# Two-layer hybrid encoder on eight cores: the tokens taken in two halves, attention of one half issued beside the dense work of the other

## The chip, the cores and the metric

One Trainium2 chip, eight cores, one program on all of them. Each core computes one of the eight batch elements on its own; the weights are the same for all. The time is the device time of the slowest core in microseconds. Kernel before: median 2806.88 us of three runs (2804.39 to 2817.87).

## The reference, cut to what matters

2064 tokens (16 learned meta tokens and 2048 of the sequence), 1024 channels, two layers, then a final RMSNorm. One layer:

```python
h = rms_norm(x, norm1_g)
q, k, v, u, gate_pre = split(h @ w_in, [512, 1024, 1536, 2048])     # u: pool input, 2048 gate channels
g_pool, g_sb = split(sigmoid(gate_pre + b_gate), 2)
a = pool_mixer(u)                       # trailing means over 2/4/8/16 tokens, minus the token, 4 small maps
s = stick_breaking_attention(q, k, v)   # 8 heads of 64; A[t,s] = beta_ts * prod_{s<j<t} (1 - beta_tj), s < t
x = x + (g_pool * (a @ w_branch_pool) + g_sb * (s @ w_branch_sb)) @ w_out
gt, up = split(rms_norm(x, norm2_g) @ w_ffn_in, 2)                  # 2 x 2816
x = x + (silu(gt) * up) @ w_ffn_out
```

Token t looks at earlier tokens only, in attention and in the pool.

## The kernel before, in words

Tokens are stored in reverse order, so the keys of a query lie at higher columns. Channels are on the partitions, tokens on the free axis. The residual `X` (float32) and the normed `H` (bf16) of all 2064 tokens stay in SBUF. `Prog` (L37) records every operation with what it reads and writes; `op` and `dma` (L94, L103) turn overlaps into semaphore waits. Each engine executes its operations in the order in which the Python code recorded them; that order is written out by hand. Weights come from HBM as float32 through POOL's DMA queue (`wdma`, L299), cast to bf16 on the way. Helpers record nearly everything: `mm` (L264) and `mmx` (L271) matmuls, `act` (L280), `tt` (L283), `stt` (L286), `cp` (L291 on ACT, L293 on DVE).

A layer runs in stages, each over all tokens before the next, in tiles of 512 tokens and one of 16 (`TT`): projections q and u with the pool mixer (`proj_fm`, `proj_u`, `pool_band`), then k and v, then `attention` (L525), then `merge_slab` (gates and branch projections, four weight slabs, L647), `out_proj` (L687) and six `ffn_slab` (L716), each slab over all token tiles, its weights loaded while the slab before it computes. The norms are taken inside `out_proj` and the last `ffn_slab`. The FFN's output is added to `X` once per slab.

`attention` cuts the work into units: one block of 128 queries, one head, one chunk of up to 7 key blocks; 224 units per layer and, in layer 0, eight more of 16 queries. A unit goes through five engines: `prep` (L558) issues the q.k matmuls on PE into one of three PSUM pairs; `core` (L576) lets ACT take the sigmoid in place, DVE scan the running product over the keys (L591), POOL subtract neighbours to get the weights (tt, L283), and SP's queue transpose them by DMA (L608, four buffers); `av` (L610) multiplies with v on PE (L624). Where a query's keys need more than one chunk, DVE copies the last product into `CAR` (L293). The loop at L636 issues `prep` two units ahead and `av` three units behind; nothing but attention is issued in this stage.

Of the kernel before, what the change touches and what calls it, by code (L numbers as in the profile page):

```python
# [11 lines left out]
D = 1024  # L12
# [7 lines left out]
TT = [(512 * i, 512 * (i + 1)) for i in range(4)] + [(2048, 2064)]  # L20
KB = [(128 * j, 128 * j + 128) for j in range(16)] + [(2048, 2064)]
CELL = 16
SUBE = 'pool'
NEG = -30000.0

# [10 lines left out]

class Prog:  # L37
    def __init__(self, nc):
        self.nc = nc
        self.ops = []  # L40
        self.cnt = {}
        self.arenas = {}
        self.alias = {}
# [4 lines left out]
    def _res(self, rs):  # L48
        out = []
        for (an, lo, hi) in rs:  # L50
            if an in self.alias:
                an, off, mul = self.alias[an]
                lo, hi = off + lo * mul, off + hi * mul
            out.append((an, lo, hi))
        return out

    def _record(self, eng, fn, reads, writes, stream, val, skip):
        need = {}
        reads, writes = self._res(reads), self._res(writes)
# [7 lines left out]
        for (an, lo, hi) in writes:  # L67
            A = self.arenas[an]
            c0, c1 = lo // CELL, (hi + CELL - 1) // CELL
            for tab in (A['W'], A['R']):  # L70
                for s, arr in tab.items():
                    v = int(arr[c0:c1].max())
                    if v > need.get(s, 0):
                        need[s] = v
        for s in skip:
            need.pop(s, None)
        for s, v in need.items():
            if s.startswith('E:'):
                assert v <= self.cnt.get(s, 0), ("dependency on a not-yet-issued inc", s, v)
# [14 lines left out]
    def op(self, eng, fn, reads=(), writes=(), inc=True):  # L94
# [3 lines left out]
        need = self._record(eng, fn, reads, writes, stream, val, skip)  # L98
        if inc:
            self.cnt[stream] = val  # L100
        self.ops.append(dict(eng=eng, fn=fn, need=need, inc=inc, dma=None))

    def dma(self, queue, fn, sem, reads=(), writes=()):  # L103
        stream = 'D:' + sem
        val = self.cnt.get(stream, 0) + 16
        need = self._record(queue, fn, reads, writes, stream, val, (stream,))
# [52 lines left out]
class Sub:  # L159
    def __init__(self, tens, off, mul=1):  # L160
        self.tens, self.off, self.mul = tens, off, mul

    def __getitem__(self, idx):
        ps_, cs_ = idx
        ap = self.tens[ps_, self.off + cs_.start * self.mul:self.off + cs_.stop * self.mul]
        return ap.bitcast(F32) if self.mul == 2 else ap

class View:
    def __init__(self, tens, name, off, A, T):
        self.tens, self.name, self.off, self.A, self.T = tens, name, off, A, T  # L170

    def ap(self, a, t0, t1, p0=0, p1=128):
        b = self.off + a * self.T
        return self.tens[p0:p1, b + t0:b + t1]

    def r(self, a, t0, t1):
        b = self.off + a * self.T
        return (self.name, b + t0, b + t1)

def build(depth=DEPTH):  # L180
    nc = bass.Bass("TRN2", target_bir_lowering=False)
    dt = nc.dram_tensor
    xT_d = dt("xT", [D, SEQ], F32, kind="ExternalInput").ap()
    meta_d = dt("metaT", [D, NMETA], F32, kind="ExternalInput").ap()
    prm_d = dt("params", [128, NPC], F32, kind="ExternalInput").ap()
    cst_d = dt("consts", [128, CO], F32, kind="ExternalInput").ap()
    w_in_d = dt("w_in", [DEPTH, D, 4096], F32, kind="ExternalInput").ap()
    pmix_d = dt("pool_mix", [DEPTH, 4, 128, 128], F32, kind="ExternalInput").ap()
    wbp_d = dt("w_branch_pool", [DEPTH, 512, D], F32, kind="ExternalInput").ap()
    wbs_d = dt("w_branch_sb", [DEPTH, 512, D], F32, kind="ExternalInput").ap()  # L190
    wout_d = dt("w_out", [DEPTH, D, D], F32, kind="ExternalInput").ap()
    wfi_d = dt("w_ffn_in", [DEPTH, D, 2 * DFF], F32, kind="ExternalInput").ap()
    wfo_d = dt("w_ffn_out", [DEPTH, DFF, D], F32, kind="ExternalInput").ap()
    y_d = dt("yT", [D, SEQ], F32, kind="ExternalOutput").ap()

    P = Prog(nc)
    with contextlib.ExitStack() as st:
# [4 lines left out]
        Xt = sb("X", 8 * NT, F32)  # L202
        PRM = sb("PRM", NPC, F32)
        ATT = sb("ATT", 20480, BF16)
        Ht = sb("H", 8 * NT, BF16)
        MIX = sb("MIX", 33488, BF16)
# [5 lines left out]
        WB, BW, FW = Sub(ATT, 0), Sub(ATT, 8192), Sub(ATT, 16384, 2)  # L212
        P.alias = dict(WB=('ATT', 0, 1), BW=('ATT', 8192, 1), FW=('ATT', 16384, 2))
        PSB = [st.enter_context(nc.psum_tensor("psb%d" % b, [128, 1024], F32)) for b in range(4)]

        class _Bank:
            def __init__(self, b):
                self.t, self.o = PSB[b // 2], (b % 2) * 512

            def __getitem__(self, idx):  # L220
                ps_, cs_ = idx
                c0 = cs_.start or 0
                c1 = 512 if cs_.stop is None else cs_.stop
                return self.t[ps_, self.o + c0:self.o + c1]

        PS = [_Bank(b) for b in range(8)]
        P.arena('ps', 8 * CELL)
        P.arena('out', CELL)

        X = View(Xt, "X", 0, 8, NT)  # L230
        H = View(Ht, "H", 0, 8, NT)
        Q = View(MIX, "MIX", 0, 4, NT)
        K = View(MIX, "MIX", 8272, 4, NT)
        V = View(MIX, "MIX", 16528, 17, 512)
        A = View(MIX, "MIX", 25232, 4, NT)
        MG = View(MIX, "MIX", 8272, 8, NT)

# [3 lines left out]
        def fw(lo, hi):  # L241
            return FW[:, lo:hi], ('FW', lo, hi)

        def bw(lo, hi):
            return BW[:, lo:hi], ('BW', lo, hi)

        IDENT = CST[:, 0:128]
        NEGM = CST[:, 128:CB]
        NEGONES = CST[:, CO:CO + 128]
        r_cst = ('CST', 0, CB)  # L250
        r_one = ('CST', CO, CO + 128)
# [667 lines left out]
```

How the kernel before makes its waits and increments, by code:

```python
            def run(ename, eng):  # L120
                waited = {}
                for o in ops:
                    if o['eng'] != ename:
                        continue
                    for s, v in o['need'].items():
                        if waited.get(s, 0) < v:
                            eng.wait_ge(sems[s], v)
                            waited[s] = v
                    if o['fn'] is None:
                        continue
                    ins = o['fn'](eng)
                    if o['dma'] is not None:
                        ins.then_inc(sems['D:' + o['dma']], 16)
                    elif o['inc']:
                        ins.then_inc(sems['E:' + ename], 1)
```

## Time and profile before

| | us |
|---|---|
| median of three runs | 2806.88 |
| profiled execution, its own time | 2806.74 |
| span of its slowest core (0) | 2804.7 |
| spans of the eight cores | 2787.2 to 2804.7 |
| PE, DVE, ACT, POOL busy | 2248.5, 1418.0, 730.2, 630.7 |
| mean granted TensorE clock of the cores | 0.816 to 0.819 |

The profile is of one execution. Busy time of an engine counts its instructions; PE and PEld (weight loads) overlap. The granted clock is a share of 2.4 GHz. A matmul's mean ns is longer than its distance from the next one, since matmuls are pipelined. Releasers (what a waiting instruction waited for) are inferred from semaphores. DMA share is the mean busy share of 16 DMA engines, GB/s what they moved (for weights, the bf16 bytes).

### The profile page before, as it was taken

How to read it: one execution, taken by the hardware profiler on the slowest of the kernel's cores; microseconds unless marked ns; L12 is line 12 of the kernel's file. 1: busy time of each engine (PE TensorE's matmuls, PEld its weight loads, DVE VectorE, ACT ScalarE, POOL GpSimd, SP SyncE). 2: the span in 40 equal slices, each digit the busy share in tenths (PEclk: the TensorE clock that was granted, in tenths of full speed). 3: DMA queues.
4: the chain of work that ended last, by engine and by line, in shares of the span. 5: the costliest groups of instructions: out<-in, count | busy, mean ns of one | idle time of the engine just before them, and what ended most of it. 6: DMA issues, size and time to landing. Idle time of an engine off the chain costs nothing.

```text
span 2804.7 us, 37292 instructions; the slowest of 8 cores (2787.2 to 2804.7 us)
## 1 busy us (share of the span) xinstructions
PE 2248.5 (80%) x10905; PEld 973.2 (35%) x11064; DVE 1418.0 (51%) x1840; ACT 730.2 (26%) x1245; POOL 630.7 (22%) x545
## 2 busy tenths in 40 slices
PE   3985665654998899999998866666589999999994
PEld 1442222221444344444444322222134444444441
DVE  3113778885343643333462267888833464433344
ACT  3312333332222211111243233333322321111132
POOL 0003666665000000000000156666610000000000
PEclk9995555555999999999999955555589999999997
DMA  6022545556222222115002044555461322221102
GB/s 160 1 30 44 88 89 97 97 96 101 32 38 38 46 46 46 16 31 77 1 1 31 10 85 85 95 102 98 90 76 23 53 45 46 46 46 19 27 27 94
DMA packets 405714, 159.56 MB, mean 57 GB/s; under 512 B 330128, under 2 KB 391568, under 8 KB 405520
## 3 DMA queue, kind: packets, MB, share of 16 engines
q1 hardware_dynamic: 335968, 96.67, 17.8%
q0 software_dynamic: 69552, 60.51, 15.0%
q8 instruction: 97, 1.59, 0.2%
q14 instruction: 97, 0.79, 0.1%
HBM read 129.51 MB, written 8.39 MB: 49 GB/s over the span
## 4 chain that ended last, share of the span: by engine, by line
PE 66%; DVE 14%; DMA 8%; issue 5%; ACT 4%; POOL 2%; SPq 1%; DVEq 0%; ACTq 0%; POOLq 0%
PE psb L264 57%; DVE ATT L591 11%; PE psb L271 5%; PE psb L624 4%; ACT psb L280 3%; DMA ATT<-ATT 3%; POOL ATT L283 2%; DMA yT<-ATT 2%; DMA X<-xT 2%; DMA ATT<-w_in 1%; DVE MIX L283 1%; SPq L608 1%; DVE H L286 1%; DMA ATT<-w_branch_sb 1%; DVEq L127 0%
## 5 line engine op out<-in xcount | busy, mean ns | idle before, releaser
L283 POOL TENSOR_TENSOR ATT<-ATT 128x768 bf16<-128x768 f32 (+6 forms) x456 | 554.5, 1219 | 339.7 <-DVE CAR L293 197.0
L264 PE MATMUL psb<-H,MIX 128*128 128x512 bf16 (+1 forms) x3098 | 626.5, 357 | 4.9 <-DVE X L283 1.1
L271 PE MATMUL psb<-MIX 64*128 64x512 bf16 (+9 forms) x824 | 330.7, 460 | 328.3 <-DVE ATT L591 325.5
L591 DVE TENSOR_TENSOR_SCAN ATT<-psb,ZF 128x770 f32<-128x770 f32 (+10 forms) x264 | 371.3, 1426 | 188.6 <-ACT psb L280 156.4
L264 PEld LDWEIGHTS psb<-H,MIX 128*128 128x128 bf16 x3168 | 286.5, 98 | 337.3 <-issue 8.9
L283 DVE TENSOR_TENSOR X<-X,psb 128x512 f32<-128x512 f32 (+1 forms) x504 | 308.8, 629 | 156.7 <-PE psb L264 156.5
L280 ACT ACTIVATE psb<-psb 128x770 f32<-128x770 f32 (+6 forms) x456 | 293.0, 671 | 314.1 <-PE psb L271 282.0
L264 PE MATMUL psb<-H,ATT 128*128 128x512 bf16 (+1 forms) x1718 | 355.5, 357 | 11.0 <-DMA ATT<-w_in 7.7
L264 PE MATMUL psb<-MIX 128*128 128x512 bf16 (+1 forms) x1569 | 329.9, 359 | 35.1 <-DVE MIX L283 34.0
L283 DVE TENSOR_TENSOR MIX<-ATT,psb 128x512 bf16<-128x512 f32 (+1 forms) x198 | 124.1, 630 | 453.1 <-PE psb L264 449.3
L280 ACT ACTIVATE ATT<-psb 128x512 f32<-128x512 f32 (+1 forms) x221 | 121.4, 550 | 821.1 <-PE psb L264 799.5
L591 DVE TENSOR_TENSOR_SCAN ATT<-psb,CAR,ZF 128x530 f32<-128x530 f32 (+4 forms) x192 | 282.4, 1522 | 6.9 <-issue 0.4
L264 PE MATMUL psb<-MIX,ATT 128*128 128x512 bf16 (+1 forms) x1138 | 238.9, 358 | 10.9 <-DMA ATT<-w_out 7.6
L271 PEld LDWEIGHTS psb<-MIX 64*128 64x128 bf16 (+1 forms) x824 | 67.1, 101 | 492.3 <-issue 467.2
L264 PEld LDWEIGHTS psb<-H,ATT 128*128 128x128 bf16 x1760 | 158.7, 99 | 195.6 <-issue 20.6
L624 PE MATMUL psb<-ATT,MIX 128*64 128x256 bf16 (+3 forms) x1288 | 180.9, 407 | 52.9 <-DMA ATT<-ATT 52.6
L264 PEld LDWEIGHTS psb<-MIX 128*128 128x128 bf16 x1584 | 142.1, 98 | 215.0 <-issue 61.5
L283 DVE TENSOR_TENSOR ATT<-ATT,psb 128x512 f32<-128x512 f32 (+1 forms) x144 | 90.3, 630 | 235.2 <-PE psb L264 234.7
L299 POOL DMA_DIRECT2D MIX<-w_ffn_in x24 | 21.2, 889 | 747.3 <-PE psb L264 747.3
L280 ACT ACTIVATE ATT<-psb,PRM 128x512 f32<-128x512 f32 (+1 forms) x144 | 91.7, 641 | 258.1 <-PE psb L264 255.5
L264 PEld LDWEIGHTS psb<-MIX,ATT 128*128 128x128 bf16 x1152 | 104.7, 99 | 133.3 <-issue 14.8
L299 POOL DMA_DIRECT2D ATT<-w_in x24 | 21.3, 893 | 567.6 <-PE psb L264 557.7
(38 smaller groups left out, 1012.8 us busy)
## 6 DMA issues: line engine op xcount, KB each, us to landing
MIX<-w_ffn_in POOLq DMA_DIRECT2D x20, 1024.0 KB, 13.0
MIX<-w_ffn_out POOLq DMA_DIRECT2D x10, 1024.0 KB, 19.6
X<-xT SPq DMA_DIRECT2D x4, 2048.0 KB, 35.3
ATT<-w_in POOLq DMA_DIRECT2D x8, 1024.0 KB, 19.7
ATT<-w_in POOLq DMA_DIRECT2D x16, 512.0 KB, 10.2
yT<-ATT SPq DMA_DIRECT2D x32, 256.0 KB, 2.5
ATT<-ATT SPq DMA_TRANSPOSE x456, 2.7
ATT<-w_out POOLq DMA_DIRECT2D x4, 1024.0 KB, 9.3
```

What stands on the lines that cost most here:

```text
L264: P.op('pe', lambda e: e.matmul(out, lhsT=lhsT, rhs=rhs, start=start, stop=stop), reads, writes, inc)
L271: P.op('pe', lambda e: e.matmul(out, lhsT=lhsT, rhs=rhs, start=start, stop=stop, skip_group_check=True), reads, writes, inc)
L280: P.op('act', lambda e: e.activation(out=out, in_=in_, func=func, **kw), reads, writes)
L283: P.op(eng, lambda e: e.tensor_tensor(out=out, in0=in0, in1=in1, op=op), reads, writes)
L286: P.op('dve', lambda e: e.scalar_tensor_tensor(out=out, in0=in0, scalar=scalar, in1=in1, op0=op0, op1=op1), reads, writes)
L299: P.dma('pool', lambda e: e.dma_start(out=out, in_=in_), sem, (), writes)
L591: P.op('dve', lambda e: e.tensor_tensor_scan(out=E, data0=za, data1=zero, initial=init, op0=ALU.mult, op1=ALU.add), r_z + [('ZF', 0, 16)] ...
L608: P.dma('sp', lambda e: e.dma_start_transpose(out=dst, in_=src), 'tw%d' % (u['n'] % 4), [r_w], wr)
L624: P.op('pe', lambda e, out=out, lh=lh, rh=rh, st_=st_, sp_=sp_, hh=hh: e.matmul(out, lhsT=lh, rhs=rh, start=st_, stop=sp_, tile_position=( ...
```

## The change

The sequence is cut into half A (columns 1024 to 2063, the earlier 1040 tokens, meta tokens included) and half B (columns 0 to 1023). Two generators yield work: `attn` gives the attention units of layer 0 A, 0 B, 1 A, 1 B, and `dense` gives everything else in the order shown. Each yields what its next piece reads and writes; the loop at the end asks a model of the engines' times, kept in `Prog` (`t`, `fin`, durations `d`), which piece would be ready, and records attention first, dense work otherwise. Tokens hold pieces back: attention of a half waits for its q projection (`Q`), gates of a half for its attention (`S`). All dense work gets three PSUM banks (eight in the last part), attention two PSUM pairs instead of three and three transpose buffers instead of four. Half A is tiled in three tiles of 346 or 347 columns where the meta tokens are needed, else two of 512.

The weights are packed on the host so that each transfer is contiguous, 2048, 1408 or 1024 elements per partition, in order of use, and pass through a ring of 8192 elements per partition; each half of each layer loads all of them again. `X` holds one half: the other is stored to HBM and loaded back on SP's queue. `H` is kept for all tokens. The FFN runs in two slabs of 11 x 128 channels, not six. Copies out of PSUM go to ACT, the sum of the two gated branches to POOL; silu is taken as sigmoid times value (ACT, ACT, POOL) except in the last part.

```diff
-TT = [(512 * i, 512 * (i + 1)) for i in range(4)] + [(2048, 2064)]
+T3 = [(1718, 2064), (1371, 1718), (1024, 1371)]
+T2 = {'A': [(1536, 2048), (1024, 1536)], 'B': [(512, 1024), (0, 512)]}
+QKV = [('k', 0, 2048), ('k', 1, 2048), ('v', 0, 2048), ('v', 1, 2048), ('q', 0, 2048), ('q', 1, 2048)]
+REST = [('u', 0, 2048), ('u', 1, 2048)]
+for _n in range(8):
+    REST += [('g', _n, 2048), ('b', _n, 1024)]
+REST += [('o', _n, 1024) for _n in range(8)]
+for _s in range(NFC // SLAB):
+    REST += [('i', _s * SLAB + _f, 2048) for _f in range(SLAB)]
+    REST += [('f', _s * 8 + _n, SLAB * 128) for _n in range(8)]
+RING = 8192
...
+    def dma(self, queue, fn, sem, reads=(), writes=(), d=1000.0):
...
+        self.tdma = max(self.tdma, t) + d
+        self.fin.setdefault(stream, []).append(max(self.tdma + 1800.0, t + 2500.0))
...
+        def w_try(force):
...
+            if not force and P.ready([], wr) > max(P.t['pe'], P.t['pool']):
+                return False
+            dst = WR[:, pos:pos + n]
+            src = w_d[l, off:off + 128 * n].rearrange("(p n) -> p n", p=128)
+            P.dma('pool', lambda e: e.dma_start(out=dst, in_=src), 'w%d' % (i % 10), [], wr, d=128 * n * 4 / 330.0)
...
             for u in units:
+                yield ('tok', ('Q', l, h, x))
+                yield u_probe(u)
+                while avq and avq[0]['n'] <= u['ch']['n'] - 2:
+                    av(avq.pop(0))
+                prep(u)
                 core(u)
...
+                def ffn_in(f, tile, s=s):
...
+                    a, ra = stg(k, N)
+                    c, rc = stg(k + 1, N)
+                    b = yield from group([(wsl(pi, kc), H.ap(kc, t0, t1)) for kc in range(8)], [ri] + h_r(t0, t1), N)
...
+                        act(a, ps(b, 0, N), AF.Sigmoid, [psr(b)], [ra], N)
+                        act(c, ps(b, 0, N), AF.Identity, [psr(b)], [rc], N)
+                        tt('pool', a, a, c, ALU.mult, [ra, rc], [ra], N)
+                    b = yield from group([(wsl(pi + 1024, kc), H.ap(kc, t0, t1)) for kc in range(8)],
+                                         [ri] + h_r(t0, t1), N)
+                    tt('dve', M_.ap(f, t0, t1), a, ps(b, 0, N), ALU.mult, [ra, psr(b)], [M_.r(f, t0, t1)], N)
...
+            yield from project(0, 'B')
+            yield from rest(0, 'A', 'sig')
+            yield from project(1, 'A')
+            yield from rest(0, 'B', 'sig')
+            yield from project(1, 'B')
+            load_pmx(1)
+            yield from rest(1, 'A', 'sig')
+            yield ('tok', ('S', 1, 'B'))
+            ps_pool[0] = list(range(8))
+            yield from rest(1, 'B', 'silu')
...
+            now = P.t['pe'] + 60.0
+            cand = []
+            if avq:
+                cand.append((P.ready(*av_probe(avq[0]), skip=('E:pe',)), 'av'))
+            for i in range(2):
+                if heads[i] is not None and heads[i][0] != 'tok':
+                    cand.append((P.ready(*heads[i], skip=('E:pe',)), i))
...
+            pick = [c for c in cand if c[0] <= now]
+            c = pick[0] if pick else min(cand, key=lambda c: c[0])
```

`project` is k, v, q of a half; `rest` is its pool mixer, the wait for `S`, gates and branches (`gate`), output (`outp`), norm, and FFN (`ffn_in`, `ffn_out`). `project(1, 'A')` first waits for attention 0 B, since K, V and Q are used again. `group` is 8 matmuls (4 for a branch, 11 for `ffn_out`) into one PSUM bank; `stg` gives two pairs of staging buffers in turn. A planned order is fixed when the program is built; on the chip each engine still executes its own list in order.

## Rows read from the trace of the kernel before

**Rows 1.** The page: busy time by engine, and PE and its clock in 40 slices of 70 us.
```profile
PE 2248.5 (80%) x10905; PEld 973.2 (35%) x11064; DVE 1418.0 (51%) x1840; ACT 730.2 (26%) x1245; POOL 630.7 (22%) x545
...
PE   3985665654998899999998866666589999999994
...
PEclk9995555555999999999999955555589999999997
```

**Rows 2.** Busy time by stretch, attention stages: stretch, length, engines, PEclk, DMA share, GB/s.
```profile
213.00:680.00 467.00, 272.30 (x1198) 97.71 (x1197) 343.02 (x331) 157.15 (x268) 283.45 (x236) 0.51 0.48 86
1597.00:2035.00 438.00, 266.41 (x1166) 94.22 (x1165) 340.92 (x322) 155.71 (x256) 279.42 (x225) 0.50 0.52 91
```

**Rows 3.** The same view, outside attention (engines: PE, PEld, DVE, ACT, POOL).
```profile
0.00:70.00 70.00, 24.28 (x85) 6.99 (x85) 23.16 (x44) 27.13 (x56) 3.41 (x8) 1.00 0.68 160
...
680.00:1526.00 846.00, 792.62 (x4309) 369.96 (x4384) 349.14 (x610) 188.19 (x336) 31.34 (x38) 0.97 0.24 35
...
2035.00:2704.00 669.00, 643.48 (x2902) 289.02 (x2963) 276.60 (x408) 122.91 (x195) 30.32 (x37) 0.99 0.27 40
2704.00:2804.70 100.70, 57.33 (x245) 24.86 (x247) 44.44 (x64) 30.45 (x45) 0.00 (x0) 0.78 0.23 84
sum 1899.70, PE 1709.80 PEld 781.26 DVE 734.07 ACT 417.39 POOL 67.79; mean PE 284.97 PEld 130.21 DVE 122.35 ACT 69.56 POOL 11.30
```

**Rows 4.** The chain that ended last, by engine, and one dense piece: start, length, what.
```profile
PE 66%; DVE 14%; DMA 8%; issue 5%; ACT 4%; POOL 2%; SPq 1%; DVEq 0%; ACTq 0%; POOLq 0%
...
2061.13 10.74 PE psb L264 x49
```

**Rows 5.** Timeline around two attention units of 770 columns: start, length, engine, line, operation.
```profile
664.54 0.80 PE L271 MATMUL psb<-MIX 64*128 64x512 bf16 x2 [1.37 <-DVE ATT L591]
...
664.74 1.82 DVE L591 TENSOR_TENSOR_SCAN ATT<-psb,CAR,ZF 128x770 f32<-128x770 f32 x1
665.55 0.80 ACT L280 ACTIVATE psb<-psb 128x770 f32<-128x770 f32 x1 [1.38 <-PE psb L271]
666.66 0.15 DVE L293 COPY CAR<-ATT 128x1 f32<-128x1 f32 x1
...
666.83 1.47 POOL L283 TENSOR_TENSOR ATT<-ATT 128x768 bf16<-128x768 f32 x1 [0.70 <-DVE CAR L293]
666.91 1.82 DVE L591 TENSOR_TENSOR_SCAN ATT<-psb,CAR,ZF 128x770 f32<-128x770 f32 x1
```

**Rows 6.** Busy time by stretch: the output projection with its norms; then ten microseconds after a weight wait.
```profile
900.00:1000.00 100.00, 86.54 (x427) 39.22 (x433) 57.88 (x98) 24.68 (x43) 2.53 (x3) 0.95 0.21 32
...
880.00:885.00 5.00, 5.00 (x17) 1.93 (x16) 0.88 (x2) 0.00 (x0) 0.00 (x0) 0.66 1.31 197
885.00:890.00 5.00, 5.00 (x32) 2.40 (x31) 1.87 (x3) 1.47 (x2) 0.00 (x0) 1.00 0.20 37
```

**Rows 7.** Groups by shape (busy, mean ns): a POOL operation of 512 columns, a weight DMA's issue.
```profile
L283 POOL TENSOR_TENSOR ATT<-ATT 128x512 bf16<-128x512 f32 x16 | 16.6, 1039 | 18.6 <-DVE CAR L293 18.6
...
L299 POOL DMA_DIRECT2D MIX<-w_ffn_in x24 | 21.2, 889 | 747.3 <-PE psb L264 747.3
```

**Rows 8.** DMA queues (packets, MB, share of 16 engines), and transposes: us from issue to landing.
```profile
q1 hardware_dynamic: 335968, 96.67, 17.8%
q0 software_dynamic: 69552, 60.51, 15.0%
...
ATT<-ATT SPq DMA_TRANSPOSE x456, 2.7
```

**Rows 9.** Timeline where the first weight loads after attention meet its last transposes; transposes' landing from 660 to 690 us.
```profile
678.07 1.80 POOL L299 DMA_DIRECT2D ATT<-w_in  x2 [0.54 <-POOL ATT L283]
...
681.32 0.94 POOL L299 DMA_DIRECT2D ATT<-w_in  x1
...
686.84 1.38 PE L624 MATMUL psb<-ATT,MIX 128*64 128x256 bf16 x9 [7.05 <-DMA ATT<-ATT]
...
DMA to landing us min/median/max: 2.6/2.7/8.7
```

More of the change, by code:

```diff
@@ new lines, in wget, with wfree, x_pump @@
+        def wget(l, h, k, j):
+            i = widx[(l, h, k, j)]
+            while wstate['next'] <= i:
+                w_try(True)
+            pos, n = wpos[i]
+            return pos, ('WR', pos, pos + n)
+        def wfree(l, h, k, j):
+            i = widx[(l, h, k, j)]
+            wlive[:] = [a for a in wlive if a[0] != i]
+        xq = []
+        def x_pump(force=False):
+            while xq:
+                reads, writes, fn, sem, nb = xq[0]
+                if not force and P.ready(reads, writes) > P.t['pe']:
+                    return
+                xq.pop(0)
+                P.dma('sp', fn, sem, reads, writes, d=nb / 300.0)
@@ L523, in chunks, with geo @@
             return cuts
[L525 to L530 removed]
+        def geo(u):
+            k0, k1 = KB[u['lo']][0], KB[u['ch']['kz'] - 1][1]
+            return k0, k1, k1 - k0 + 2, KB[u['b']][1] - KB[u['b']][0]
@@ L531, in attention @@
+        def attention(l, h):
+            units = []
+            gs = (([8] if l < depth - 1 else []) + [7, 6, 5, 4]) if h == 'A' else [3, 2, 1, 0]
+            for g in gs:
                 bs = [16] if g == 8 else [2 * g, 2 * g + 1]
@@ new lines, in attn @@
+        def attn():
+            for l in range(depth):
+                for h in 'AB':
+                    yield from attention(l, h)
+        P.dma('sp', lambda e: e.dma_start(out=PRM[:, :], in_=prm_d), 'prm', (), [r_prm])
+        P.op('dve', lambda e: e.memset(CST[:, CO:CO + 128], -1.0), (), [r_one])
+        P.op('dve', lambda e: e.memset(ZF[:, :], 0.0), (), [('ZF', 0, 16)])
+        P.op('dve', lambda e: e.memset(Kt[:, 0:16], 0.0), (), [('K', 0, 16)])
+        P.op('dve', lambda e: e.memset(Wt[:, :], 0.0), (), [('W', 0, 3072)])
@@ new lines, in build, with settle, advance @@
+        for k, (t0, t1) in enumerate(T3):
+            x_load_tile('A', 2 + k, t0, t1)
+        x_pump(True)
+        wget(0, 'A', 'k', 1)
+        P.dma('pool', lambda e: e.dma_start(out=CST[:, 0:CO], in_=cst_d[:, 0:CO]), 'cst', [], [('CST', 0, CO)])
+        load_pmx(0)
+        streams = [attn(), dense()]
+        heads = [next(s) for s in streams]
+        def settle(i):
+            while heads[i] is not None and heads[i][0] == 'tok' and heads[i][1] in tokens:
+                advance(i)
+        def advance(i):
+            try:
+                heads[i] = next(streams[i])
+            except StopIteration:
+                heads[i] = None
```

1131 lines of the change are left out of this document (545 added, 586 removed).

## The prediction, made before the changed kernel was run

> **What bounds the kernel now.** I read the page first. PE is busy 80% of the span, but its clock row stands at half in two runs of seven slices [rows 1]: these are the attention stages. So the next view is busy time by stretch. In the two attention stages (467 and 438 us, 905 together) the granted clock is 0.50, that is 1.2 GHz, and PE is busy for 272 and 266 us, 60% of the time; DVE is the busiest with 343 and 341 [rows 2]. Outside them PE is 94 to 96% busy in the long stretches at 0.97 and 0.99, that is 2.4 GHz, and DVE under half [rows 3]. The chain agrees: 66% PE, 14% DVE, 8% DMA; a dense piece of it is 49 matmuls in 10.74 us, 219 ns each [rows 4]. The timeline of an attention unit shows its pace: scan 1.82, carry copy 0.15, the next scan 2.17 us after the last one, while q.k (0.80), sigmoid (0.80) and subtraction (1.47) lie beside it [rows 5]. So the kernel is two programs in turn: PE alone at full clock for 1900 us, and DVE's scan for 905 us with PE waiting at half clock.
>
> **The change, term by term.** *PE work.* Dense work keeps its matmuls: 1710 us [rows 3]. Three tiles of 347 columns instead of two of 512 and one of 16: 219 ns less 213 (512 columns at 2.4 GHz) leaves 6 fixed, so 3 x 150 = 452 against 438 and the small tile; I count nothing, with 15 us either way. Attention's 539 us were taken at half clock [rows 2]; at 2.4 GHz they are about 269. Sum 1979. Whether the clock stays up is a bound: 269 or 539, and half speed for what lies beside it (third rival); I take 269, since a stretch 87% busy ran at 0.95 and after a weight wait the clock was back at 1.00 within ten microseconds [rows 6].
>
> *What lies beside what.* A quarter (half the tokens, one layer) is 427 us of dense PE work. By matmuls per 512 tokens (96 for q, k, v; about 40 for u and pool; 784 for gates, branches, output, FFN) that is 45, 19 and 364 us. Attention of A has 27% of the key columns (36 us of PE, 0.27 x 438 = 118 us of time today), B 73% (98 and 320). In order: k, v and the first q of A with its norms, 39 us, alone. Attention 0 A beside the rest of q, B's projections and A's pool: 114 us of PE against 118 of scans; this stretch is DVE's, and I add 25 us of PE idle. Attention 0 B beside rest 0 A: 462. Project 1 A 45 alone, then attention 1 A beside rest 0 B and project 1 B: 464. Attention 1 B beside rest 1 A: 481. Rest 1 B alone: 383. That is PE's 1979 us again, with 320 us of scans to hide in more than 460, so DVE stops being the bound.
>
> *Ends.* Today PE has 24 us of work in the first 70 [rows 3], 46 idle; three smaller loads and fewer weights before the first matmul, but also three norms before k: between 30 and 65, I take 50. The tail today has 43 us without PE in its last 101 [rows 3]; the last norm now writes into X itself and waits for no staging buffer, but the norm, its stores and their landing remain: 20 to 43, I take 30. So 1979 + 25 + 50 + 30 = 2084.
>
> *Stalls of PE in the planned order.* Alone (467 us) it loses 4% as in 2035 to 2704 [rows 3], 20 us. In the three mixed stretches (1407 us) it waits in order on ACT, DVE, POOL and DMA. No stretch of today is like it; the nearest are that 4% (55 us) and the output projection with its norms, 87% busy, which loses 16% (220 us) [rows 6]. I take 9%, 125 us: closer to the second would be right if the order were written by hand, but a piece is only placed where the model has it ready. Sum 2084 + 20 + 125 = 2229.
>
> *Costed at nothing, and the cover.* DVE in the largest mixed stretch: 0.73 x 342 = 250 of attention, and 234 dense operations of 347 columns at about 0.5 us, 117; 367 in some 500 us. The four FFN slabs saved, 256 adds over the two layers, and the copies moved to ACT lighten DVE where it is not the bound: nothing. POOL: 0.73 x 281 = 205 [rows 2], 90 sums and products at 0.70 (1039 ns for 512 columns) and 68 weight issues at 0.89 [rows 7], in all 328. In order behind a weight issue stand the subtractions; it waits for a ring slot only where PE lags the plan, and then attention waits with it. By the code 280 weight DMAs take the place of 80; if nothing hid them, 200 x 0.89 = 178 us of POOL. Two PSUM pairs: 0.40 + 0.80 + 1.97 and handoffs, some 3.4 us per pair, so 1.7 per unit under the 2.17 of DVE; with a dense group (8 x 0.219 = 1.75) in front of each q.k it is 2.6 per unit, 144 x 2.6 = 374, still inside 500. DMA: weights today 60.5 MB in 15.0% of the span, 0.144 MB/us [rows 8]; the mixed stretch of rest 0 A loads 28.8 MB, 200 us. Transposes of B, 29 MB at 86 / 0.48 = 179 GB/s [rows 2], 163 us; x out and back, 8.5 MB at 160 / 0.68 [rows 3], 36 us. In all 399 of 500: covered, but with little left, and it is second after PE. The x transfers stand on SP's queue ahead of transposes; were one planned 3 us too early, three subtractions would wait for it.
>
> *Transposes meeting weights.* They land after 2.7 us today, almost all without weights beside them [rows 8]. The one collision is after attention: with five weight DMAs issued from 678 to 682 us a transpose took 8.7, and PE stood for 7.05 [rows 9]. A load of 2048 elements (0.52 MB) takes 3.6 us at 0.144 and is wanted every nine, so weights flow 40% of the time; a transpose that meets one load lands by 6.3. Bounds 2.7 and 8.7; mean about 4.1, nearer to the first, since loads come singly. With three buffers a unit takes (landing + 1.47 + 0.3) / 3: 2.0 us at 4.1, 282 for B's 144 units, no cost.
>
> The profiled execution took 2806.74 us, 2 above its span and equal to the median of 2806.88 within 0.2; so the sum gives 2229 + 2, **2230 us**, 577 below.
>
> **Rivals.** *First: the planned order does not fit and PE waits in it.* A product of the FFN passes ACT twice, POOL and DVE: 2 x 0.45 + 0.70 + 0.5 and handoffs, 2.5 us, and up to 0.80 + 1.47 + 1.82 more where an attention operation stands in front on each. PE can run ahead by three banks, 3.6 us with 347 columns. Half of the worst gap of 3 us on 66 products is 99 us, some 30 elsewhere; with 16% for the other stalls the time is 2084 + 20 + 220 + 130 = 2454. For it: every queue is in order, two staging pairs. Against: the model knows these queues, and attention fills gaps. Case: 2310 to 2700.
>
> *Second, ending slower: transposes starve behind the weights.* Place: SP's DMAs in all four attentions, buffers W. If every transpose lands as the one at 678 us did, a unit takes 3.49 us. PE's list was laid out for some 330 us per attention of B, 143 and 150 for A, so the stretch grows by 2 x (144 x 3.49 - 330) + 88 x 3.49 - 143 + 80 x 3.49 - 150 = 638: 2868 us. It decides from a mean landing of 8.3 us, where the extra is 577. For it: rows 9, and weights flow during every attention now. Against: five loads were queued there, and the ring holds four units, one or two of them in use. The Trainium skill, page "DMA: Bandwidth & Descriptors", section "Queues, rings and completion order", has each DMA engine take turns between queues packet by packet. By that rule the packed weights, in pieces of up to 4096 bytes instead of 870, would hold a transpose of 34 packets per engine (157 KB on average, in packets of 288 bytes) for about 15 us while loads are queued, an estimate from that page: 0.4 x 15 + 2.7, a mean landing of about 8.8, and a time near 2890. Rows 9 agree in direction; no run here shows the larger packets.
>
> *Third, also slower: the clock.* Where PE waits so much that it falls to 1.2 GHz, each microsecond of its work costs one more. It decides where 577 of the some 1520 us of work beside attention run at half. For it: 60% busy ran at 0.50 [rows 2]. Against: these stretches need PE over 85% busy.
>
> *Fourth: nothing gained*, because tokens and waits put the halves one after another again: about 2807.
>
> **Chances.** Forecast, 2090 to 2310: 0.60. First rival 0.26. Second 0.09, third 0.03, fourth 0.02. Half a percent, 14 us, is about what a measurement of this kernel can tell from no change. Faster 0.86, same 0.02, slower 0.12. The range reaches from the lower bounds (mixed stalls at 4%, start and tail at their least: 2230 - 70 - 20 - 10 = 2130, less 40 if the small tiles and the attention matmuls, packed between others, cost less than counted) to the middle of the first rival's case: 2090 to 2560; it leaves out 0.14 above for the others and a few hundredths of the first rival.
>
> **What would show it.** Right: PEclk at 0.9 or more in all mixed slices; PE 85 to 95% busy in them; DVE 70 to 75%; the chain over 80% PE; attention 0 B ending well before rest 0 A; transposes landing in 4 to 5 us. Wrong by the first rival: PE's idle ahead of dense groups released by DVE or POOL; by the second: PE's av matmuls and POOL's subtractions waiting for DMA, landing over 8 us; by the third: slices at 0.5. The sum is wrong if PE's busy time comes out far from 1980, or if loads of weights end PE's waits.

## The result, and the profile after

| | before | after |
|---|---|---|
| median us (of 4 runs each) | 2812.38 | 2543.16 |
| ratio, with its 95% interval | | 0.9039 [0.8998, 0.9079] |
| profiled execution, its own time | 2806.74 | 2533.05 |
| span of its slowest core | 2804.7 (core 0) | 2531.5 (core 4) |
| mean granted TensorE clock of the cores | 0.816 to 0.819 | 0.925 to 0.929 |

The kernel became 269 us faster where 577 were forecast; 2543 lies inside the range, near its slow end. Disturbed runs count in the medians but not in the ratios, so the ratio is the number to compare; e6 and e15 had too few others for one, and their lowest run is given.

The page of the changed kernel: busy time, PE and its clock in 40 slices (63 us each), the DMA queues and the chain. Lines of this kernel: L308 every matmul, L297 two-tensor operations, L290 and L294 ACT, L301 the norm's last product, L346 weight DMAs, L462 the scan, L480 the transposes.

```profile
PE 2133.5 (84%) x11096; PEld 991.0 (39%) x11096; DVE 1146.3 (45%) x1394; ACT 862.7 (34%) x1497; POOL 954.7 (38%) x969
...
PE   1888689857788989898899989996888995989994
...
PEclk9988689978999999898999999998999998999997
...
q0 software_dynamic: 41520, 120.29, 29.5%
...
PE 58%; DMA 14%; DVE 10%; issue 6%; ACT 5%; POOL 5%; SPq 1%; DVEq 0%; POOLq 0%; ACTq 0%
...
L346 POOL DMA_DIRECT2D WR<-weights x280 | 155.6, 559 | 624.4 <-PE psb L308 606.7
```

Against [rows 1] the two runs of seven slices at half clock are gone and DVE fell from 1418 to 1146 us. But PE's row still has sixes, sevens and eights, and PE is 58% of the chain, not over 80.

Busy time by stretch: length, PE, PEld, DVE, ACT, POOL, then PEclk, DMA share, GB/s.

```profile
0.00:105.00 105.00, 48.06 (x256) 25.88 (x257) 15.59 (x32) 30.43 (x65) 6.66 (x18) 1.00 0.58 127
105.00:330.00 225.00, 166.15 (x815) 68.92 (x814) 110.45 (x122) 99.25 (x193) 87.94 (x97) 0.75 0.50 89
330.00:960.00 630.00, 523.98 (x3270) 291.31 (x3269) 361.92 (x452) 229.38 (x413) 307.31 (x294) 0.93 0.57 95
500.00:700.00 200.00, 135.75 (x767) 69.61 (x766) 114.45 (x127) 72.67 (x124) 88.06 (x74) 0.85 0.45 74
960.00:1510.00 550.00, 505.84 (x2435) 222.86 (x2433) 197.47 (x252) 183.25 (x325) 192.47 (x214) 0.95 0.54 95
1510.00:2100.00 590.00, 529.36 (x2666) 220.04 (x2664) 354.55 (x380) 232.36 (x365) 308.41 (x271) 0.96 0.64 107
2100.00:2531.00 431.00, 360.12 (x1662) 162.01 (x1660) 106.30 (x156) 88.03 (x137) 51.90 (x76) 0.93 0.42 83
```

In 500 to 700, output projection and FFN of A beside attention of B, PE is 68% busy and DVE 57%: nobody is the bound. PE's busy time times the granted clock, summed over slices of 10 us, is its work at full clock: 2023 us. Busy time less that, 110, is what the clock cost; span less busy, 398, is idle. The forecast had 1979 of work, no clock loss and 250 of idle (25 + 50 + 30 + 20 + 125). The miss in the span, 2531 less 2229 = 302, is thus 44 of work, 110 of clock and 148 of idle. Idle time is read directly; the split between work and clock is rough, to some 70 us: the same sum gives 1953 of work for the kernel before and 1946 for e6, which has the changed kernel's matmuls.

What PE waited for (us in total, times, longest), and two waits of DVE and POOL:

```profile
PE psb L308 <- ACT H L290: 106.0, 14, 40.9
PE psb L308 <- DMA WT<-W: 89.1, 47, 6.5
PE psb L308 <- DVE E L462: 73.6, 53, 10.7
PE psb L308 <- DVE RA L297: 50.8, 35, 3.1
PE psb L308 <- ACT STG L294: 29.4, 9, 24.8
PE psb L308 <- DMA WR<-weights: 6.2, 2, 3.8
...
DVE RA L297 <- POOL STG L297: 252.5, 102, 4.0
...
POOL W L297 <- DMA WT<-W: 149.6, 57, 8.8
```

Weights hardly end a wait of PE. Norms (H; the start is in it), transposes (WT), scans (E) and FFN products (RA) do.

### The profile page after: what moved, and what is told of

It is laid out like the page before. It is cut to its first block, busy times and chain, and to the rows that moved or that the text cites. A ratio compares the mean times of both kernels' runs of the same rounds, so it can differ in the third digit from the quotient of the medians.

```text
span 2531.5 us, 38757 instructions; the slowest of 8 cores (2512.6 to 2531.5 us)
## 1 busy us (share of the span) xinstructions
PE 2133.5 (84%) x11096; PEld 991.0 (39%) x11096; DVE 1146.3 (45%) x1394; ACT 862.7 (34%) x1497; POOL 954.7 (38%) x969
## 3 DMA queue, kind: packets, MB, share of 16 engines
q0 software_dynamic: 41520, 120.29, 29.5%
## 4 chain that ended last, share of the span: by engine, by line
PE 58%; DMA 14%; DVE 10%; issue 6%; ACT 5%; POOL 5%; SPq 1%; DVEq 0%; POOLq 0%; ACTq 0%
PE psb L308 58%; DMA WT<-W 10%; DVE E L462 6%; POOL W L297 3%; DVE H L301 2%; DMA yT<-X 2%; ACT psb L290 2%; DMA X<-xA 1%; POOL STG L297 1%; ACT H L290 1%; SPq L480 1%; DVE X L297 1%; ACT L290 1%; ACT RS L290 1%; DVE RA L297 0%
## 5 line engine op out<-in xcount | busy, mean ns | idle before, releaser
L308 PE MATMUL psb<-H,WR 128*128 128x512 bf16 (+2 forms) x4960 | 1023.6, 363 | 50.3 <-DVE RA L297 49.4
L297 POOL TENSOR_TENSOR W<-E 128x768 bf16<-128x768 f32 (+6 forms) x456 | 553.9, 1220 | 662.5 <-DVE E L462 300.2
L308 PEld LDWEIGHTS psb<-H,WR 128*128 128x128 bf16 x4960 | 480.9, 100 | 540.1 <-issue 105.2
L462 DVE TENSOR_TENSOR_SCAN E<-psb,ZF 128x770 f32<-128x770 f32 (+10 forms) x264 | 375.8, 1431 | 368.1 <-ACT psb L290 308.4
L308 PE MATMUL psb<-RA,WR 128*128 128x512 bf16 (+2 forms) x2160 | 447.5, 365 | 9.9 <-POOL RA L297 4.8
L290 ACT ACTIVATE psb<-psb 128x770 f32<-128x770 f32 (+6 forms) x456 | 303.4, 675 | 294.1 <-PE psb L308 236.3
L346 POOL DMA_DIRECT2D WR<-weights x280 | 155.6, 559 | 624.4 <-PE psb L308 606.7
L290 ACT ACTIVATE STG<-psb 128x512 f32<-128x512 f32 (+2 forms) x352 | 175.2, 543 | 515.0 <-PE psb L308 460.7
L462 DVE TENSOR_TENSOR_SCAN E<-psb,CAR,ZF 128x530 f32<-128x530 f32 (+4 forms) x192 | 293.2, 1534 | 92.7 <-ACT psb L290 67.4
L297 DVE TENSOR_TENSOR RA<-STG,psb 128x512 bf16<-128x512 f32 (+2 forms) x198 | 124.6, 630 | 440.4 <-POOL STG L297 252.5
L308 PEld LDWEIGHTS psb<-RA,WR 128*128 128x128 bf16 x2160 | 210.1, 100 | 231.2 <-issue 35.3
L308 PE MATMUL psb<-K,Q 64*128 64x512 bf16 (+9 forms) x824 | 234.9, 330 | 75.2 <-DVE E L462 73.6
L297 POOL TENSOR_TENSOR STG<-STG 128x512 f32<-128x512 f32 (+2 forms) x154 | 172.9, 1123 | 165.7 <-ACT STG L290 163.3
L297 DVE TENSOR_TENSOR X<-X,psb 128x512 f32<-128x512 f32 (+2 forms) x216 | 134.5, 628 | 203.7 <-PE psb L308 199.8
L290 ACT ACTIVATE H<-X 128x512 bf16<-128x512 f32 (+2 forms) x184 | 103.2, 574 | 292.5 <-DVE X L297 290.1
L308 PE MATMUL psb<-WT,V 128*64 128x256 bf16 (+3 forms) x1288 | 120.2, 292 | 89.3 <-DMA WT<-W 89.1
L290 ACT ACTIVATE STG<-psb,PRM 128x512 f32<-128x512 f32 (+2 forms) x144 | 92.2, 641 | 179.1 <-PE psb L308 169.0
L308 PE MATMUL psb<-H,CST 128*128 128x512 bf16 (+2 forms) x184 | 58.6, 484 | 106.0 <-ACT H L290 106.0
L308 PEld LDWEIGHTS psb<-K,Q 64*128 64x128 bf16 (+1 forms) x824 | 61.9, 94 | 219.3 <-issue 196.4
L301 DVE SCALAR_TENSOR_TENSOR H<-X,PRM,RS 128x512 bf16<-128x512 f32 (+2 forms) x152 | 97.1, 712 | 110.5 <-ACT RS L290 110.4
L308 PE MATMUL psb<-WR,H 128*128 128x512 bf16 (+1 forms) x544 | 135.3, 404 | 6.2 <-DMA WR<-weights 6.2
L297 DVE TENSOR_TENSOR STG<-STG,psb 128x512 f32<-128x512 f32 (+2 forms) x144 | 86.8, 621 | 104.5 <-ACT STG L290 98.2
```

The source lines that it names most:

```text
L290: P.op('act', lambda e: e.activation(out=out, in_=in_, func=func, **kw), reads, writes, d=0.83 * N + 190)
L297: P.op(eng, lambda e: e.tensor_tensor(out=out, in0=in0, in1=in1, op=op), reads, writes, d=(1.67 * N + 185) if eng == 'pool' else (1.05 * N ...
L301: P.op('dve', lambda e: e.scalar_tensor_tensor(out=out, in0=in0, scalar=scalar, in1=in1, op0=ALU.mult, op1=ALU.mult), reads, writes, d=1.0 ...
L308: P.op('pe', lambda e: e.matmul(out, lhsT=lhsT, rhs=rhs, start=start, stop=stop, **kw), reads, writes, inc, d=max(N, 64) / 2.4 + 6 if d is ...
L346: P.dma('pool', lambda e: e.dma_start(out=dst, in_=src), 'w%d' % (i % 10), [], wr, d=128 * n * 4 / 330.0)
L462: P.op('dve', lambda e: e.tensor_tensor_scan(out=E, data0=za, data1=zero, initial=init, op0=ALU.mult, op1=ALU.add), r_z + [('ZF', 0, 16)] ...
```

## Two theories of the missing gain

**R, rings.** Timeline of A's FFN (start, length, engine, operation, and in brackets idle time before it and its releaser):

```profile
621.05 1.75 DVE L462 TENSOR_TENSOR_SCAN E<-psb,ZF 128x770 f32<-128x770 f32 x1
...
623.02 1.46 POOL L297 TENSOR_TENSOR W<-E 128x768 bf16<-128x768 f32 x1 [2.03 <-DVE E L462]
...
624.45 0.90 POOL L297 TENSOR_TENSOR STG<-STG 128x346 f32<-128x346 f32 x1
...
625.52 0.52 DVE L297 TENSOR_TENSOR RA<-STG,psb 128x346 bf16<-128x346 f32 x1 [2.46 <-ACT psb L290]
625.96 1.75 DVE L462 TENSOR_TENSOR_SCAN E<-psb,ZF 128x770 f32<-128x770 f32 x1
...
626.19 2.52 PE L308 MATMUL psb<-H,WR 128*128 128x347 bf16 x16 [1.88 <-DVE RA L297]
```

The scan releases the subtraction on POOL; behind it on POOL stands silu's product (STG); that releases the FFN's product on DVE (RA); and behind that on DVE stands the next scan. Data alone do not lead round: the order of POOL's and DVE's queues closes the ring. The product's inputs were there when ACT had ended, at 623.7; it starts at 624.45, when the subtraction ends. (RA's wait is put down to attention's sigmoid, which ended within 0.1 us of STG; over the whole kernel DVE waits 252.5 us for STG there.) PE's next q.k stands behind the group that waits for RA, so the sigmoid is no way around. One turn takes 625.96 - 621.05 = 4.9 us, one unit per turn instead of one per 2.17 [rows 5], and PE waits 1.88 in each.

In A's output projection there is a second one:

```profile
507.55 2.12 DVE L462 TENSOR_TENSOR_SCAN E<-psb,CAR,ZF 128x914 f32<-128x914 f32 x1 [1.84 <-ACT psb L290]
...
509.59 0.49 DVE L297 TENSOR_TENSOR X<-X,psb 128x347 f32<-128x347 f32 x1
...
510.23 0.49 ACT L290 ACTIVATE H<-X 128x347 bf16<-128x347 f32 x1 [2.85 <-DVE X L297]
...
511.89 0.92 ACT L290 ACTIVATE psb<-psb 128x914 f32<-128x914 f32 x1
512.98 2.12 DVE L462 TENSOR_TENSOR_SCAN E<-psb,CAR,ZF 128x914 f32<-128x914 f32 x1 [1.64 <-ACT psb L290]
```

Scan, adds to X behind it on DVE, the squares for the norm on ACT (two of each, one is shown), attention's sigmoid behind them on ACT, next scan: 5.4 us.

**D, transfers.** Transposes land later while weights are loading, and attention and its av matmuls hold PE's list up (89.1 us for WT, and 149.6 of POOL). The median landing was 2.7 [rows 8], the longest 8.7 in the stretch of [rows 9]. From issue to landing in the changed kernel:

```profile
DMA to landing us min/median/max: 2.2/3.1/11.0
```

The median hides the spread. Counted one by one in the traces, 181 of the 456 transposes took more than 4 us, where 20 did before, and the mean rose from 2.84 to 4.12 us. Those with no weight load under way between issue and landing (198) took 3.05 on average; those with one, two, or three and more took 4.3, 5.4 and 6.1. Of PE's 89.1 us of waits for WT, 80.7 end with a transpose that took more than 4 us.

A rival to both is that running the halves together gains nothing in itself (what is left of the gain would be the packed weights and fewer FFN slabs). In the runs below "worth" is the ratio's difference to 0.9039, times 2806.88. The interval of that 0.9039 is 11 us on either side; those of the runs are 5 to 32 us, and both count in a difference.

## Experiments

**Is it the overlap?** e6 lets attention go first: dense work is not recorded while an attention piece is at hand (and K is set to zero as a whole).

```diff
+            if any(c[1] != 1 for c in cand):
+                cand = [c for c in cand if c[1] != 1]
```

> Two halves, ring of weights, three tiles and all edits as in the changed kernel, but dense work is placed only where attention has nothing left to place: attention and dense work in turn, half by half. It tells what the overlap is worth in the changed kernel, whose other edits then stand alone. If the overlap carries the whole gain: about the time of the kernel before, 2800 us and more, since the attention stretches again have PE at 1.2 GHz (905 us before) and two PSUM pairs instead of three. If the other edits (fewer FFN additions, copies on ACT, packed weights) carry part of it: 2650 to 2750.

Lowest of four runs 2947.08, median 3010.11, beside a lowest of 2806.24 for before. PE idles 686 us, 397.2 of it for scans, and the clock costs 315.

```profile
PE   2655765557989987669899975555798999598994
...
PEclk9755755557999997559999985555799999899997
...
PE psb L308 <- DVE E L462: 397.2, 292, 6.4
```

Slower than before: the fives of the attention stages are back. The overlap carries the whole gain, and more than 400 us (2947 - 2533); without it the other edits together are 141 us slower than the kernel before.

**Ring one, opened on POOL.** e1 takes silu's product from PSUM on DVE, so that POOL's queue is out of the ring.

```diff
-                        act(c, ps(b, 0, N), AF.Identity, [psr(b)], [rc], N)
-                        tt('pool', a, a, c, ALU.mult, [ra, rc], [ra], N)
+                        tt('dve', a, a, ps(b, 0, N), ALU.mult, [ra, psr(b)], [ra], N)
```

> Silu of the FFN beside attention is taken as one ACT sigmoid and a DVE product with the value in PSUM; the second ACT pass and POOL's product go. Theory R (a ring of in-order queues: scan, then POOL's subtraction, then POOL's product behind it, then DVE's product behind that, then the next scan behind it, 4.9 us a unit in the changed kernel at 605 to 640 us): the ring opens, units go to about 3 us in the FFN stretches, attention 0 B and 1 B end some 80 us earlier each, and the kernel takes 2450 to 2500 us. Theory D (transposes wait behind weights): no change beyond 10 us, 2535 to 2550. Theory C (the clock falls by itself in the mixed stretches): no change of PE's granted clock, mean 0.926.

2501.95; 0.8913 [0.8876, 0.895]: worth 35 us, 2 us outside theory R's range and far from D's. The wait for RA, 50.8, is gone from PE's list; that for WT is 99.1. The last scans of attention 0 B and 1 B start 44 and 55 us earlier, not 80.

**Ring one, opened on DVE.** e3 records the FFN's last product one piece later, so that the next scan stands in front of it.

```diff
+                    mul_flush()
                     b = yield from group([(wsl(pi + 1024, kc), H.ap(kc, t0, t1)) for kc in range(8)],
-                    tt('dve', M_.ap(f, t0, t1), a, ps(b, 0, N), ALU.mult, [ra, psr(b)], [M_.r(f, t0, t1)], N)
+                    mulq.append(('dve', M_.ap(f, t0, t1), a, ps(b, 0, N), ALU.mult, [ra, psr(b)],
+                                 [M_.r(f, t0, t1)], N))
```

> Same instructions as the changed kernel, but DVE's last product of an FFN item is recorded one group later, so that a scan recorded in between stands ahead of it. Theory R: it is the order alone that closes the ring, so this gains most of what taking POOL out of it gains: 2460 to 2510 us. If the load on POOL is what counts and not the order: 2530 to 2550. Theory D: 2535 to 2550.

2542.96; 0.9023 [0.8973, 0.9073]: 4 us, nothing that can be told, where theory R had 33 to 83 us. PE's wait for RA fell as meant, but that for scans rose by 23:

```profile
PE psb L308 <- DVE E L462: 96.6, 69, 10.7
...
PE psb L308 <- DVE RA L297: 4.0, 9, 1.0
```

The ring itself did open. Scans from 640 to 740, beside the FFN of A, in the changed kernel and then in e3 (stretch, length, DVE busy in scans with their number, PEclk, DMA share, GB/s):

```profile
640.00:740.00 100.00, 39.74 (x25) 0.93 0.44 78
...
640.00:740.00 100.00, 66.58 (x43) 0.92 0.71 108
```

A unit takes 2.3 us there, not 4.0, so the order alone does close the ring. The last scan of attention 0 B starts at 756 instead of 818; but attention 1 A, which waits for the dense work of A, begins at 981 instead of 989. A slow attention was therefore not a cost in itself here: what counts are PE's waits, and from the start of 0 B to that of 1 A these fell only from 112 to 98 us.

**Ring two.** e2 records the norm's square three items later (`sq_flush(k)` takes squares from the list `sqq` until k are left; the same in the last `ffn_out`), so that attention's sigmoid stands in front of it on ACT.

```diff
-                square(X_, n, t0, t1)
+                sqq.append((X_, n, t0, t1))
+                sq_flush(3)
```

> The squares behind the output projection and behind the last FFN slab are recorded three items later, so that ACT's next sigmoid of attention does not stand behind a square that waits for an addition on DVE that stands behind a scan. Theory R (the second ring, 4.5 to 5.4 us a unit at 500 to 530 us and at 1700 to 1730): units there go to about 3 us, and each of the two stretches of some 60 us loses 15 to 20: 2500 to 2520 us. Theory D: 2535 to 2550.

2504.91; 0.8917 [0.8888, 0.8946]: 34 us. PE's wait for scans fell from 73.6 to 41.0, for RA to 42.6. But the units did not go to 3 us: the 18 units at the output projection and its norm took 83 us (from 493), where they had taken 95 (from 498), 4.6 each for 5.3. So the ring was opened in part.

**The gap at 2100.** Late in the kernel PE stands for 24.8 us, and the chain to it is a buffer: the pool's output of the last half lies in X, which the stores of A's final output are still reading.

```profile
2125.08 0.69 ACT L290 ACTIVATE X<-psb,PRM 128x512 bf16<-128x512 f32 x1 [26.07 <-DMA yT<-X]
...
2126.50 0.59 PE L308 MATMUL psb<-STG,PMX 128*128 128x512 bf16 x1 [24.79 <-ACT STG L294]
```

e5 puts that output into WT, which attention no longer needs.

```diff
+            if l == depth - 1 and h == 'B':
+                o = c * 1024
+                return WTt[:, o + t0:o + t1], ('WT', o + t0, o + t1)
```

> In the last quarter the pool mixer writes into the transposes' buffer, free by then, and not into the part of X whose last rows are still being stored. The gap of PE at 2100 to 2125 us, released by the stores, should go: 2510 to 2525 us. If the loads of X behind the same stores end the gap next, little changes: 2530 to 2545.

2517.83; 0.8961 [0.8916, 0.9007]: 22 us; the wait for STG on ACT is 4.4 instead of 29.4.

**Together.** e7 is e1 + e2 + e5, e8 is e3 + e2 + e5.

> The product of the FFN on DVE, the squares three items late and the pool's output in the transposes' buffer together. Theory R: the two rings and the gap are different stretches, so the gains add: some 60 + 30 + 20 us, 2420 to 2450. If opening a ring only moves the wait to the next resource (transposes, PSUM banks): 2470 to 2510.

> As the combination before, but with the FFN's last product one group late instead of on DVE: POOL and ACT keep their work. Theory R: within 20 us of that combination, 2420 to 2470. If POOL's load is a bound of its own: 2480 to 2520.

e7: 2474.71; 0.8789 [0.8674, 0.8904], 70 us (32 on either side), with parts that make 35 + 34 + 22 = 91, and outside the 2420 to 2450 of theory R. e8: 2461.18; 0.8762 [0.8737, 0.8788], 78 us, inside its 2420 to 2470. The parts of e8 make 4 + 34 + 22 = 60 one by one. That the late product is worth some 20 once the others are in is not shown: the intervals that enter here come to some 30 us. Ring one is open in e8; in the output projection there are 23 scans in 100 us instead of 20, and PE's largest wait is the transposes (the first line is of the changed kernel, the others of e8):

```profile
500.00:600.00 100.00, 38.17 (x20) 0.80 0.39 66
...
500.00:600.00 100.00, 43.77 (x23) 0.78 0.48 82
...
PE psb L311 <- DMA WT<-W: 114.5, 58, 7.5
...
PE psb L311 <- DVE E L465: 56.3, 52, 4.6
...
PE psb L311 <- DVE RA L300: 5.3, 11, 2.3
```

**Transfers.** e4 loads an eighth of each weight piece, all issues, waits and sizes of matmuls staying as they are; past the first four pieces the rest of a slot keeps older weights.

```diff
+            nn = n if i < 4 else n // 8
-            dst = WR[:, pos:pos + n]
-            src = w_d[l, off:off + 128 * n].rearrange("(p n) -> p n", p=128)
+            dst = WR[:, pos:pos + nn]
+            src = w_d[l, off:off + 128 * n].rearrange("(p n) -> p n", p=128)[:, 0:nn]
```

> After the first four pieces only an eighth of each weight piece is loaded (the products are then of old weights); every wait stays. Theory D: transposes land as without weights (2.7 instead of 3.1 us, the slowest 4 instead of 11), PE's 89 us of waits for them go, and with them POOL's 150: 2420 to 2470 us. Theory R: only those of PE's waits go that are not on a ring, most of them in attention 0 A and 1 A, 15 to 40 us: 2500 to 2530.

2429.94; 0.8652 [0.8632, 0.8671]: 109 us, in theory D's range. Only the bytes are gone (17.5 MB instead of 120), and with them most of the waits for WT, 149.6 to 48.4 us on POOL and 89.1 to 18.1 on PE; those of the rings stay (PE waits 55.5 for RA and 77.3 for scans).

```profile
  POOL W L297: 48.4, 25
  PE psb L308: 18.1, 19
...
DMA to landing us min/median/max: 2.2/2.8/10.3
```

The landing's median moved by 0.3 us only and its longest, expected at 4, hardly at all. The cost is in the many late ones, which PE meets in order: 41 of 456 took more than 4 us, not 181. e12 is e4 + e8:

> An eighth of each weight piece after the first four (products of old weights), and the late product, the late squares and the pool's output in the transposes' buffer. If the rings of queues and the transposes behind weights are two separate causes, the gains add: 2543 - 113 - 82 = 2350 us, within 20. If they are one wait seen twice: 2400 to 2430. What is then left above 2230 is neither: start, norms at the joints, the clock.

2373.32, lowest 2345.73; 0.8338 [0.8277, 0.8399]: 197 us, where 78 and 109 make 187. The two add (e8's share holds the 22 us of the gap besides the rings). In its profile (span 2344.2) idle is 262, the clock costs 66, and the work is 2016.

**Why do weights delay transposes?** e9 cuts the weights into packets of 512 to 704 bytes, not 2048 to 4096, and packs them on the host to match.

```diff
+            m = 352 if n == 1408 else 256
+            dst = dst.rearrange("p (a m) -> p a m", m=m)
-            src = w_d[l, off:off + 128 * n].rearrange("(p n) -> p n", p=128)
+            src = w_d[l, off:off + 128 * n].rearrange("(a p m) -> p a m", p=128, m=m)
```

> The weights are packed so that each transfer is cut into rows of 256 or 352 elements (512 or 704 bytes written) instead of one row of up to 4096 bytes per partition; same bytes, same order, same waits. If it is the length of a weight packet that holds a transpose up (the DMA engines take turns by packet), transposes get more turns: PE's 89 us of waits for them halve and the kernel takes 2470 to 2510 us. If it is the weights' bytes in front of them, however cut, nothing changes: 2530 to 2550; and if small packets make the weights themselves slow, more waits for weights (6 us now) and 2550 to 2600.

2538.92; 0.9022 [0.8934, 0.911]: 5 us, nothing that can be told (25 us on either side).

```profile
q0 software_dynamic: 226864, 120.29, 38.1%
...
  PE psb L308: 84.3, 46
...
DMA to landing us min/median/max: 2.2/3.1/12.0
```

5.5 times the packets, the same landing: that the length of these packets sets what a transpose waits is not borne out. Two things stay open. The smaller packets also made the weights' own traffic heavier, a load taking 7.0 us to land on average instead of 6.1, so a gain and a loss may hide each other. And what the profile counts as packets are single pieces, some nine to each of the 16 engines in one load. The Trainium skill, page "DMA: Bandwidth & Descriptors", section "Queues, rings and completion order", has an engine change queues at packet bounds only, and by a packet it means a bundle of descriptors; no run here shows whether e9 made such bundles shorter.

e11 gives POOL a fourth buffer W (the ring of weights 7872 elements instead of 8192, for space).

```diff
-            wo = (u['n'] % 3) * 1024
+            wo = (u['n'] % 4) * 1024
```

> Four transpose source buffers instead of three, paid for with a ring of 7872 instead of 8192 elements. If POOL's 150 us of waits for a transpose to give its buffer back are what slows attention under the weights: those waits fall to about 60 and the kernel takes 2490 to 2515 us. If PE's av matmuls, which need the transposed data itself, are what counts: 2525 to 2550, POOL's waits gone all the same.

2550.37; 0.9036 [0.8939, 0.9134]: nothing that can be told (27 us on either side), though POOL's wait fell from 149.6 to 59.6. PE's wait for transposes stayed at 85.3, so it does not come from POOL's delay. With the smaller ring PE's wait for weights rose from 6.2 to 22.0, and a gain of that size may be hidden.

**The plan.** The model lets a transfer land 2.5 us after its issue, and before each unit it records the av of two chunks ago without asking whether its transposes are ready. e14 asks (`av_probe`); e15 asks, and lets transposes land after 5 us in the model; e16 is e15 + e8. Nothing that the engines compute or move is changed by these, only the order.

```diff
+                while avq and avq[0]['n'] <= u['ch']['n'] - 2:
+                    n0 = avq[0]['n']
+                    yield av_probe(avq[0])
+                    if avq and avq[0]['n'] == n0:
+                        av(avq.pop(0))
                 yield u_probe(u)
-                while avq and avq[0]['n'] <= u['ch']['n'] - 2:
-                    av(avq.pop(0))
...
-        self.fin.setdefault(stream, []).append(max(self.tdma + 1800.0, t + 2500.0))
+        self.fin.setdefault(stream, []).append(max(self.tdma + 1800.0, t + (5000.0 if sem.startswith('tw') else 2500.0)))
```

> The placing of av alone, with the landing left at 2.5 us. It tells how much of the run before comes from the forced av and how much from the landing in the model. If the forced av counts: 2500 to 2525 us; if the landing counts: 2530 to 2550.

> Only the plan: the model lets a transpose land after 5.0 us instead of 2.5, and an av that must come before the next unit of attention is placed when the model has its transposes landed, not at once. If the transposes behind weights cost what they do because PE's list was laid out for landings of 2.5 us: PE's 89 us of waits for them fall to about 40 and the kernel takes 2490 to 2515 us. If attention itself is held up (it has to wait for them wherever av stands): 2535 to 2550, with the waits moved to the scan and to subtraction.

> The same plan on top of the late product, the late squares and the pool's output in the transposes' buffer, whose PE waits 115 us for transposes. By the first of the two readings: 2400 to 2435 us, below every version so far; by the second: 2455 to 2470.

e14: 2529.33; 0.8984 [0.8954, 0.9014], 15 us; PE's wait for WT 71.7. e15: lowest 2495.31 (the profiled one; median 2567.14) beside 2533.05 for the change's lowest and 2516.51 for e14's, with that wait at 25.6. So asking and the longer landing each seem to give about half, though for e15 this is one run. e16: 2422.03 (2418.75 to 2424.51); 0.8621 [0.8602, 0.864], 117 us better than the change and 40 better than e8. It is the fastest version that loads all weights.

```profile
PE psb L311 <- DVE E L465: 111.1, 89, 7.2
...
PE psb L311 <- DMA WT<-W: 26.5, 19, 3.8
```

The waits for WT fell by 88 from e8's, those for scans rose by 55: units placed later would end later, and some 40 of D's 109 come back through the plan.

## Why the prediction missed by half

**Right.** The mechanism, by e6. PE's work: 2023 for 1979, by a rough sum. The price of 150 ns for a matmul of 347 columns held:

```profile
505.85 1.33 PE L308 MATMUL psb<-RA,WR 128*128 128x346 bf16 x8 [0.25 <-DVE X L297]
...
510.91 2.54 PE L308 MATMUL psb<-RA,WR 128*128 128x347 bf16 x16
```

Eight more take 1.21 us, 151 ns each; 2.54 / 16 would count the end of the last one too. DVE is no longer the bound. Weights end only 6.2 us of PE's waits, and a weight issue costs POOL 0.56 us, not 0.89.

**Right in part by luck.** 960 to 1510 took 550 for 551: the idle time is as forecast, 44, but 20 of clock stand against less work. The last quarter, 2100 to 2531, took 431; 383 + 20 + 30 = 433 were forecast: its idle time is 71 where some 46 were allowed, 25 of it the gap at 2100, and its work is 355, not 383.

**Wrong, the stalls.** The step that failed is "I take 9% [...] but a piece is only placed where the model has it ready". From 330 to 2100 PE is idle for 106 + 44 + 61 = 211 us where 125 were forecast, and beside attention 0 A (105 to 330) for 59, not 25. The loop asks about the matmuls of a piece; what a piece then puts on ACT, POOL and DVE goes behind whatever stands there, and no piece is asked whether attention's next scan is behind it. So the two rings came, and the scans of attention 0 B ran from 322 to 818, 496 us, not 320 to 374 (e3 shows that this pace cost little by itself; PE's waits cost). Forecast by stretch and measured, clock included: 105 to 330, 139 and 225; 330 to 960, 504 and 630; 1510 to 2100, 524 and 590; that holds 278 of the 302. (The prediction's stretches of PE work add to 1988, not to the 1979 that it names.) The first rival named this path (twice ACT, POOL, DVE) and its case holds the result; its 130 us for the FFN were more than ring one gave up (35 by e1), and the output projection, which it counted in the 16%, had a ring of its own.

**Wrong, transposes.** "282 for B's 144 units, no cost" failed. The mean landing came out as I had it, 4.12 for 4.1, and partly by luck: 57% of the transposes met a load, not 40%, and one that did lost 1.9 us on average, not 3.6. Yet weights cost 109 us (e4). What failed is the step from the mean to "no cost": I priced buffers (a fourth one gave nothing that can be told, e11) and left out that PE takes the late transposes in the order of a plan that has them land in 2.5; a better plan gave some 40 back (e16). The second rival's place was right and its price, 638, about six times too high. Its estimate of a mean landing of 8.8 counted single pieces as packets; 4.12 was measured.

**Wrong, the clock.** I counted none of it lost beyond what 1710 us of dense work already held, some 28 by the same sum; 110 us were. Of these 34 fell between 100 and 330, beside attention 0 A (0.75 there). Over the kernels it goes with idle time: 315 at 686 of idle (e6), 110 at 398, 104 at 337 (e8), 66 at 262 (e12). On average a missed stall thus cost a quarter to a third more than itself below 400 us of idle. No run changed idle time alone, and e8, with 61 us less of it than the changed kernel, gave back only 6 of clock; so this is a relation over kernels and not a price.

With rings, gap and transfers all taken out, in part at least (e12), the idle time is 262 and the forecast's was 250; what then remains of 2344 against 2229 is 66 of clock, 37 of work, 12 of idle. So these three account for the stalls in sum.

**Open.** Attention of 0 A is slow even in e12, where PE is 79% busy at 0.78 from 100 to 300: its scans wait for sigmoids there (84.4 us in the change's 105 to 330), and whether the norms of B that stand beside them on DVE and ACT or the small units are the reason was not tried. Norms (H) end 91 to 120 us of PE's waits in every version. Of D, the part that the plan does not give back was not followed further, and no run tells by what means a weight load makes a transpose late.

```profile
100.00:300.00 200.00, 157.38 (x806) 66.32 (x804) 107.23 (x121) 98.38 (x194) 84.42 (x97) 0.78 0.41 78
```

## What to carry to other kernels

When two streams of work share in-order queues, look for rings: follow the operations behind each releaser until the path comes back to the engine where it began, and record the link whose result is needed last a piece later. Opening a ring may speed up the stream that it held and leave the time where it was (e3), so look whose waits the time hangs on, and try several together as well. A planner is only as good as the latencies that it is given and the places where it is asked; take these from the trace with all traffic present, and take their spread and not only the median. Count stalls with what the clock adds to them.

## Unexpected of the hardware

Weights in 5.5 times as many packets (e9) left the transposes' landing at 3.1 us (mean 4.05 for 4.12) while the queue's own share rose from 29.5% to 38.1%. On POOL a product took 0.92 us with 346 or 347 columns and 1.28 with 512, where the subtraction of neighbours took 1.04 with 512 [rows 7]: the forecast's 0.70 was scaled from an operation that is cheaper per column. Contiguous weights were issued in 0.56 us, strided ones before in 0.89 [rows 7].
